# Attention rounds of four tiles and two score steps, on four score banks

## The reference

```
h = rmsnorm(x, g)
z = h @ w_in
y_lru = rg_lru(causal_depthwise_conv(u_lru, conv_w, conv_b), ...)
o_cmp, p_cmp = cmp_attention(q, compress(kc), compress(vc))   # 31 compressed blocks
o_slc = slc_attention(q_rot, rope(ks), vs, idx, ok)           # selected blocks
o_win = win_attention(q_rot, rope(kwn), vwn)                  # window of 512
y_nsa = gates[0] * o_cmp + gates[1] * o_slc + gates[2] * o_win
y = concat(y_lru * silu(g_lru), y_nsa * silu(g_nsa))
return x + y @ w_out
```

## Time and profile before

| | us |
|---|---|
| median of 3 runs | 549.22 (549.05 to 549.28) |
| the profiled execution's own time | 550.92 |
| its span, first to last instruction | 549.1 |
| attention of layer 0, from the second score step to the last `W` | 139 to 246 |
| attention of layer 1 | 404 to 527 |

### The profile page before, as it was taken

One profiled execution on the slowest core, in us unless ns is written; L12 is line 12 of the kernel. 1 busy time (PEld: TensorE's weight loads), 2 busy tenths in 40 slices (PEclk: granted clock), 3 DMA queues, 4 the chain that ended last, 5 costly groups with the idle time before them and its releaser, 6 DMA issues.

```text
span 549.1 us, 8550 instructions
## 1 busy us (share of the span) xinstructions
PE 529.4 (96%) x3055; PEld 389.4 (71%) x3055; DVE 397.2 (72%) x633; ACT 293.3 (53%) x595; POOL 87.5 (16%) x105
## 2 busy tenths in 40 slices
PE   8999999999999999899999999999999998999995
PEld 7777868778666656558887787777776665666674
DVE  3596996789977787754747499668978689569642
ACT  5756733626666555533634773562475554446532
POOL 4101101120111011103520110013111111113000
PEclk9999999999999999999999999999999999999999
DMA  9776483455212433412333846626432233112113
GB/s 268 204 214 174 96 206 84 103 119 143 70 34 52 102 73 78 99 36 75 84 95 95 218 124 156 125 59 142 108 116 65 62 87 82 34 40 59 38 39 115
DMA packets 108186, 57.25 MB, mean 104 GB/s; under 512 B 42721, under 2 KB 106353, under 8 KB 108145
## 3 DMA queue, kind: packets, MB, share of 16 engines
q1 hardware_dynamic: 104992, 52.25, 37.9%
q0 software_dynamic: 1536, 3.15, 2.4%
q10 hardware_dynamic: 1616, 1.32, 0.8%
HBM read 44.12 MB, written 2.10 MB: 84 GB/s over the span
## 4 chain that ended last, share of the span: by engine, by line
PE 64%; DVE 18%; issue 6%; SPq 5%; DMA 3%; ACT 3%; POOL 1%; POOLq 0%; DVEq 0%; ACTq 0%
PE z_ps L1630 10%; PE z_ps L1632 10%; PE z_ps L1631 10%; PE s_ps L1706 5%; PE o_ps L1771 3%; PE o_ps L1630 3%; PE t_ps L1729 3%; PE o_ps L1632 3%; PE o_ps L1631 3%; PE a_ps L1771 3%; DVE mn L1512 2%; DMA probsT<-swp 2%; DVE probs L1396 2%; PE t_ps L1734 2%; DVE w_lo L1224 1%
## 5 line engine op out<-in xcount | busy, mean ns | idle before, releaser
L1152 ACT ACTIVATE probs<-s_ps,mn 128x128 f32<-128x128 f32 (+3 forms) x128 | 66.7, 527 | 76.1 <-DVE mn L1512 75.6
L1630 PE MATMUL z_ps<-h_hi,w_hi 128*128 128x512 f32 x248 | 101.3, 409 | 0.0
L1632 PE MATMUL z_ps<-h_hi,w_lo 128*128 128x512 f32 x248 | 97.0, 391 | 0.0
L1631 PE MATMUL z_ps<-h_lo,w_hi 128*128 128x512 f32 x248 | 96.8, 390 | 0.0
L974 ACT ACTIVATE w_hi<-stage 128x1024 fp32r<-128x1024 f32 x54 | 57.3, 1060 | 60.4 <-PE z_ps L1632 35.4
L1512 DVE TENSOR_REDUCE mn<-s_ps 128x1 f32<-128x384 f32 (+3 forms) x88 | 52.3, 636 | 30.7 <-PE s_ps L1714 30.5
L939 POOL TENSOR_TENSOR w_lo<-stage,w_hi 128x1024 fp32r<-128x1024 f32 x13 | 31.2, 2401 | 180.6 <-ACT w_hi L974 180.6
L1630 PEld LDWEIGHTS z_ps<-h_hi,w_hi 128*128 128x128 f32 x248 | 46.6, 188 | 14.0 <-issue 4.2
L1224 DVE TENSOR_TENSOR w_lo<-stage,w_hi 128x1024 fp32r<-128x1024 f32 x41 | 50.1, 1222 | 5.5 <-ACT w_hi L974 4.8
L1632 PEld LDWEIGHTS z_ps<-h_hi,w_lo 128*128 128x128 f32 x248 | 46.5, 188 | 10.3
L1631 PEld LDWEIGHTS z_ps<-h_lo,w_hi 128*128 128x128 f32 x248 | 46.7, 188 | 8.4 <-issue 0.2
(11 more groups left out here) (248 smaller groups left out, 984.3 us busy)
## 6 DMA issues: line engine op xcount, KB each, us to landing
stage<-in_w_in SPq DMA_DIRECT2D x27, 512.0 KB, 4.1
stage<-in_w_in SPq DMA_DIRECT2D x34, 256.0 KB, 3.9
probsT<-swp SPq DMA_DIRECT2D x112, 64.0 KB, 2.1
stage<-in_cmp_k_w SPq DMA_DIRECT2D x8, 512.0 KB, 4.0
stage<-in_cmp_v_w SPq DMA_DIRECT2D x8, 512.0 KB, 4.2
stage<-in_w_out SPq DMA_DIRECT2D x8, 512.0 KB, 3.5
stage<-in_w_out SPq DMA_DIRECT2D x16, 256.0 KB, 4.0
swp<-E POOLq DMA_DIRECT2D x48, 64.0 KB, 2.3
```

The lines of the kernel that those rows point to most:

```text
L1152: act.activation(probs[:, 4 * pair + 2 * g + r, c0:c0 + W], s_ps[g][:, at * W:(at + 1) * W], ACT.Exp, scale=-1.0, bias=mn[:, m % 2, g, at: ...
L1630: pe.matmul(bank, w_hi[:, slot, at:at + P], x_hi, start=first, stop=False)
L1631: pe.matmul(bank, w_hi[:, slot, at:at + P], x_lo, start=False, stop=False)
L1632: ins = pe.matmul(bank, w_lo[:, slot, at:at + P], x_hi, start=False, stop=last)
```

## The change

The attention stage is written anew. `tile_rounds`, `SECONDS` and `put_later` go; `SETS` holds twelve sets of four tiles, and a round now has four tiles and two score steps `a` and `b`. The two steps of a round use different banks: `a` uses both `s_ps`, `b` uses `z_ps[1]` and `t_ps[1]`. That leaves one bank, `z_ps[0]`, for pieces and one, `t_ps[0]`, for turns; the last two sets may also turn into both `s_ps`. The first tile of ten sets a layer goes by `D` (issued by SP at a step of its own, `DX`), the other 38 are turned by TensorE and all copied by ScalarE. All `w_lo` of this stage are made by VectorE, none by GpSimd. `probsT` has four slots and two areas for coefficients. The probabilities that a round computes are turned two rounds later. The order of all small steps is given by tables and by the place in the round.

```diff
-N_STAGE, N_RING, N_PT, N_FAR, N_E, N_SWP = 4, 3, 2, 2, 6, 2
+N_STAGE, N_RING, N_SLOT, N_E, N_SWP = 4, 3, 4, 6, 2
...
+N_START = KT
+PIECES = (((8, 4),) + ((4, 0),) * 9 + ((2, 0), (0, 0)), ((8, 4), (4, 4)) + ((4, 0),) * 10)
...
+GATED_AT = {6: 0, 8: 1, 10: 2}
...
+SETS = tile_sets()
+FAR = {tiles[0] for tiles in SETS[2:]}
...
+    add(("S", step))
+    close()
+    add(("MX", step, 0), ("MX", step, 1))
+    split("HI")
+    add(exps(step, 0), exps(step, 1), *tanhs, ("CS2",), *silus)
...
+        for at, turn in enumerate(turns):
+            add(turn)
+            if at == 0:
+                if late:
+                    add(late)
+                add(*(("O", *group) for group in ended(n - 1) if group not in COEFS_AT[n]))
+                add(*(("K", *group) for group in COEFS_AT[n]))
+            if at == 1:
+                add(*tanhs)
+                if n < len(SETS) and SETS[n][0] in FAR:
+                    add(("D", SETS[n][0]))
+                add(*silus)
+                tanhs, silus = [], []
+                if n in GATED_AT:
+                    add(("Y", GATED_AT[n]), ("YH", "n", GATED_AT[n]))
+            fill(share[at])
...
+            add(("S", a), ("MX", a, 0), ("MX", a, 1))
+            close()
+            add(("S", b), ("MX", b, 0), ("MX", b, 1), exps(a, 0), exps(a, 1), exps(b, 0))
+            late = exps(b, 1)
...
+        add(*rest, *(("W", key) for key in tiles))
...
+        score_banks, turn_banks = [s_ps, [z_ps[1], t_ps[1]]], [t_ps[0], *s_ps]
...
+            if plan.turn_bank[n]:
+                eng.wait_ge(exp_ok, plan.exps[per_layer(plan.steps, plan.turns[n][0] + 1) - 1])
...
-                    if plan.low[split][0] == "pool":
-                        hi, lo = split_into(split)
-                        pool.wait_ge(hi_split, hi_count(split))
-                        pool.tensor_tensor(lo, stage_of(plan.split[split]), hi.bitcast(F32), ALU.subtract).then_inc(low_pool, 1)
...
-                elif kind == "T":
-                    key = (st[1], *st[2])
-                    if key[1] != "B" and st[2] in SECONDS:
-                        n, rows = turn_no[key], P if key[1] == "P" else NC
-                        dve.wait_ge(t_full, n + 1)
-                        dve.tensor_copy(probsT[0:rows, wait_near_slot(dve, key), :], t_ps[n % 2][0:rows, :]).then_inc(pt_dve, 1)
...
-                if m >= 1:
-                    pe.wait_ge(exp_ok, plan.exps[m])
+                if m >= 2:
+                    pe.wait_ge(exp_ok, plan.exps[m - 1])
+                if m == per_layer(plan.steps, l) + 1:
+                    who, count = plan.freed(plan.z, plan.z_before[l])
+                    pe.wait_ge(z_free[who], count)
+                    pe.wait_ge(gates_read, 4 * CT * (l + 1))
```

More of the change, by code:

```diff
@@ L136, in attention, with add @@
         pieces += [("G", l, t, c, p) for t in range(TT - 1) for c in range(2) for p in range(CT)]
-    taken = 0
+    steps = score_steps()[1:]
+    s, taken, closing, splits, tanhs, silus, finals = [], 0, [], 0, [], [], []
+    def add(*some):
+        s.extend((st[0], l, *st[1:]) for st in some)
     def fill(n):
-        nonlocal taken
-        out = []
+        nonlocal taken, splits
         for st in pieces[taken:taken + n]:
-            out.append(st)
+            s.append(st)
             if st[0] == "G":
@@ L151, in fill @@
+                splits += st[2] == KT - 1
+                splits += st[1:] == (("OL", DEPTH - 1, KT // 2 - 1), KT - 1)
         taken += n
[L152 to L205, removed]
@@ L207, in attention @@
-    ahead = score_steps()
-    turned = {key[1:4]: n for n, tiles in enumerate(rounds) for key in tiles if key[0] == "P"}
-    def score(n):
-        if not ahead:
-            return []
-        if any(turned[unit] > n for b, pair, _ in parts(ahead[0]) for unit in probs_before(ahead[0][0], b, pair)):
-            return []
-        return [ahead.pop(0)]
-    def exps(step):
-        return [("EX", l, step, n) for n in range(2)]
-    ahead.pop(0)
-    second = ahead.pop(0)
-    s = [*fill(2), ("TURN", l, LAST), ("TURNE", l, LAST), *fill(FIRST_PIECES[l] - 2), ("S", l, second), ("MX", l, second, 0),
-         ("MX", l, second, 1), *fill(SECOND_PIECES), *exps(second), ("CS2", l)]
@@ L245, in attention, with close, split, exps @@
-    return put_later(s + fill(len(pieces)))
+    def close():
+        for st in closing:
+            add(st)
+            if st[0] == "FE":
+                tanhs.append(("TANH", st[1]))
+                silus.append(("SG", st[1]))
+            if st[0] == "GE" and st[2] == 1:
+                add(("FMEAN", st[1]))
+                finals.append(("FSCALE", st[1]))
+        closing.clear()
+    def split(kind):
+        for _ in range(splits):
+            add((kind,))
+    def exps(step, half):
+        return ("EX", step, half)
@@ new lines, in ended @@
+    def ended(n):
+        last = {}
+        for at, tiles in enumerate(SETS):
+            for key in tiles:
+                last[(key[1], 2) if key[0] == "C" else key[1:3]] = at + 1
+        return [group for group in GROUPS if last[group] == n]
+    step = steps.pop(0)
+    fill(2)
+    add(("TURN", LAST), ("TURNE", LAST))
+    fill(N_START - 2)
+    add(("S", step))
[3 more added lines that the diff above has]
+    add(exps(step, 0), exps(step, 1), *tanhs, ("CS2",), *silus)
@@ L248, in schedule @@
+    i = TT - 1
+    add(*(("O", *group) for group in ended(len(SETS))), ("Y", i), ("YH", "n", i), ("YL", "n", i))
+    while taken < len(pieces):
+        fill(CT if taken % CT == 0 else CT - taken % CT)
+        split("HI")
+        lows, splits = splits, 0
+        close()
+        add(*(("LO",) for _ in range(lows)))
+        if len(finals) > 1:
+            add(finals.pop(0))
+    add(*finals)
+    return s
 def schedule():
@@ L1366, in _ @@
                 if kind in ("ON", "LO") and split < len(plan.split):
[L1367 to L1368 removed]
+                    split_lo(split)
                     split += 1
```

250 lines of the change are left out of this document (123 added, 127 removed).

## The result

The changed kernel takes **557.5 us** (median of 4 runs, 556.0 to 558.3) against 549.25 for the kernel before (median of 4, 549.05 to 550.3): a ratio of 1.0143, 95% interval 1.0117 to 1.0169. It is slower by some 8 us. The prediction said slower and named 551.9; it missed by 5.6 us, and the time lies above its range.

A forecast was written before the change was run, and what follows sets the result against it. TensorE, busy 96%, was taken to bound the kernel through its waits. New waits +16.1, matmuls 0 and removed waits -13.3 gave +2.8 us, added to the median 549.22 and rounded down: 551.9 us, range 547.6 to 555.6.

The forecast's parts named there:

- the cost in matmuls: TensorE in attention: eight more turned tiles cost 4.1 us, fewer weighing groups save 3.8; taken as 0, between -2 and +2.
- What the change removes: TensorE's waits in both attention stages and one clock fall: all 13.3 us gone, at the least half, 6.7.
- VectorE at nothing: VectorE gains 17 splits of 1.22 us, loses 20 copies and eight transposes; these balance, so costed at nothing.
- The new waits: TensorE waiting in attention, mostly for ScalarE's copies of turned tiles: +16.1 us together.
- fourth tile, rounds 1 and 2: Last weighing waits 1.4 us for a copy behind six exponentials, four times in all: +5.8 us (3 to 8).
- opening: Second turn of each layer waits 1.7 us for ScalarE's copy of the first: +3.4 us (2 to 4).
- one-piece gaps and `YH`: 24 turns one piece apart wait 0.15 us each, +3.6; `YH` delays third copies in rounds 6, 8, 10, +1.8.
- bank of the first chunk: Layer 0: the second score step waits for the first chunk's bank to be evicted: +0.8 us.
- second turn of round 11: Layer 0: this turn needs `s_ps`, so it waits for the very last exponential: +0.7 us.
- The third, that the clock falls in the new waits: Rival: TensorE's new waits of 1.4 to 1.7 us bring falls costing 1.7 us each; two give 555 us; chance 0.1.
- The first rival: ScalarE reaches the opening and fourth-tile copies a microsecond sooner, shrinking those waits to 1.4 and 1.8 us; 546 us; chance 0.2.
- the fourth, VectorE: Rival: VectorE is half a microsecond late in each of 16 long rounds, 8 us; 560 us; chance 0.05.

The follow-up runs named there:

- b_dve: The kernel before with one part of the change alone: VectorE makes every `w_lo` of attention, GpSimd none; 546.35 us, ratio 0.9922.
- a_pool: The changed kernel with one part undone: GpSimd makes the `w_lo` of attention again; 557.7 us, ratio 1.0134.
- e_fourth: The changed kernel with the fourth tile of rounds 1 and 2 turned between the two score steps, so copied before the six exponentials; 548.45 us, ratio 0.9963.
- e_open: The changed kernel with ScalarE's copy of each layer's first turned tile ahead of the second score step's exponentials; 554.3 us, ratio 1.0082.
- e_cover2: The changed kernel with unread extra matmuls in TensorE's long idle times: 13 at each of six places, 16 at the far tile; 554.3 us, ratio 1.0077.
- e_b_far: The changed kernel with coefficient turns of rounds 3, 4, 6, 8, 10 between score steps and the last round's far tile weighed last; 554.35 us, ratio 1.0062.
- e_4_shift8: e_fourth with 8 extra matmuls of 256 bf16 columns before layer 0's attention opening; 549.8 us, ratio 0.9996.
- e_4_shift: e_fourth with 16 extra matmuls of 256 bf16 columns before layer 0's attention opening; 550.5 us, ratio 1.0004.

## Why the prediction was wrong, point by point

**What bounds the kernel** was right in the main: waits of TensorE and its clock account for every experiment. Between the two kernels the spacing of the matmuls moved the time too, see the cost in matmuls.

**What the change removes.** The waits of score steps went, all of them. Their size, 11.6 us, can be checked only together with the cost in matmuls: the changed kernel's span without falls, 552.6, less its new waits of 19.3 (below) is 533.3; the kernel before, 549.05 less 1.0 for its fall less 11.6, is 536.4. The step that failed in the sum is the next one. I took 1.7 us for the fall of the clock out of the profiled span, and then laid the sum on the median of 549.22. But that median was of runs without this fall: the time of a run stands 1.7 to 2.3 us over its span, mostly 1.8, so 549.2 is a span of some 547.4 (an inference, since no clock is known of those three runs), while the profiled 549.1 held the fall. In 21 later runs of the kernel before, seven spans lie at 547.2 to 548.0 with a clock of 0.998 or 0.999, and all but one of the others at 548.5 to 549.9 with 0.994 to 0.998. So **the same 1.7 us were taken off twice.** "Profiling adds about 1.7 us outside what changes" was the wrong reading of a difference that was the clock itself. Half of its length was also too much for this fall: it cost 1.0 us (b_dve).

**The cost in matmuls**, 0 between -2 and +2: the two sums above leave -3.1 us. Added up by starts and less waits and falls, over both layers, turns take 3.2 us more (forecast 4.1) and weighing 2.4 less (forecast 3.8). A term was missing: the score steps take 20.1 and 20.3 us a layer in the kernel before and 18.9 in the changed one, where two of them follow each other without other work between, 2.6 less. That is -1.8 counted and -1.3 not placed, so the cost lay at the low bound or beyond it. VectorE at nothing: right, by b_dve and a_pool, but for the far tile below.

**The new waits**, 16.1 us, were measured at 19.3, which the matmuls' -3.1 cancels by luck:

| place | forecast | measured | by |
|---|---|---|---|
| fourth tile, rounds 1 and 2 | 5.8 | 6.2 | e_fourth |
| opening | 3.4 | 3.8 | e_open |
| one-piece gaps and `YH` | 3.6 + 1.8 | 3.8 + 2.6 | starts in e_cover2: 18 waits of 0.16 and six of 0.46 to 0.82; moving 20 turns gave 3.6 back |
| bank of the first chunk | 0.8 | 0.8 | timeline after: 10.96 us between two score steps, 10.11 in layer 1 |
| second turn of round 11 | 0.7 | 0 | timeline after |
| far tile of round 12 | none | 2.1 | idle time and its edge; e_b_far gave 1.05 back |

The last row was missed. I had written that a far tile is sent a round ahead, and didn't follow VectorE's queue in round 11 of layer 0, where the transpose stands behind a `w_lo` of 1.22 us, two outputs and the coefficients, with no pieces left to cover the DMA:

```profile
247.60 0.43 DVE L1548 COPY probsT<-coef 128x512 f32<-128x512 f32 x1
247.94 1.10 DVE L1534 STREAM_TRANSPOSE swp<-probs 128x512 f32<-128x512 f32 x1
```

In round 11 the last exponential was in time, so that 0.7 never came.

**The rivals.** The third, that the clock falls in the new waits, is what happened, and it had 0.1. It was argued from one row: waits of 1.3 us brought no fall, one of 2.18 did. The sum took six new waits of 1.4 to 1.7 us, between the two, and put nothing in for the clock; this is the second step that failed, and the larger one, 3.2 us by e_cover2. There were seven such waits, with the far tile's 2.0. Its price of two falls, 3.4 us, was a fair estimate. The first rival (ScalarE reaches the copies sooner) is out: the fourth tile's copy in round 1 ran from 4.96 to 5.55 us after the score step's start, as laid out, and the second turn of the opening came at 6.4 instead of 6.2 us. So is the fourth, VectorE. Beside the third rival stood a rule of the Trainium skill ("TensorE: Matmul & The Clock Gate", section "A second HAM failure mode: psum-queue depth-cycling"), by which the many short waits on one bank would make the clock swing. The trace agrees with the row and not with it at this size: e_cover2 has all 24 waits on that bank (0.16 us, and six of up to 0.8) and no fall in attention, and in every profile the falls in attention began in or within 2 us behind an idle time of 1.5 us or more.

**The sum of the error.** Laid on the profiled execution's own time, 550.9, with what was measured, the sum is 550.9 - 11.6 - 1.0 + 19.3 - 3.1 = 554.5 us (-3.1 is itself what was left of two such sums), against 554.3 measured without falls in e_cover2. The forecast of 551.9 lacked 1.7 by the base, 0.7 by the price of the old fall, 0.1 by rounding and 0.1 by new waits and matmuls together, which were each 3 us off in opposite directions. The falls in the new waits add 3.2. Of what the prediction said would show it, all waits were found at their places, with 1.56 us at the fourth tiles (idle time and its edge) for 1.4 and 1.86 at the opening for 1.7, and score steps no longer wait for exponentials.

## What to carry to other kernels

When a wait is traded for another, write down what stands ahead of the releasing instruction in its engine's queue: here four copies behind six exponentials each, and two behind eight, with the falls that came at them, ate what a better layout had won, and moving them ahead, with three smaller moves, made the kernel 2.2% faster than the old one. Before subtracting a disturbance that a profiled execution shows, see whether the median has it at all, by comparing the granted clock and span of each run. And price an idle time of TensorE of 1.5 us or more, as they were here, with a chance of a fall of the clock on top of its length.

## What the runs showed of the hardware

- The lower clock costs at most half its length: 1.0, 1.2, 1.4, 1.6 and 1.7 us for falls of 3.4 us, 2.7 and 2.9 for 6.8, each as the difference of the same stretch with and without it.
- An idle time of 2.0 us with the same matmuls around it was followed by a fall in one profiled execution (e_4_shift8) and by none in two (e_fourth, e_4_shift); idle times of 1.0 to 1.3 us (the kernel before, b_dve) were followed by none. With the idle times filled by matmuls that nothing reads there was no fall before the program's end in the profile of e_cover2, and the clock was 0.998 or 0.999 in its five runs.
- Score steps that follow each other directly take less of TensorE's time than single ones: 18.9 us a layer instead of 20.1 and 20.3.
- VectorE's operation on 128x8 elements, stretched to 1.85 and 2.36 us by a `w_lo` of GpSimd in one order, took 0.43 us at most in another with the same 17 operations on GpSimd: whether the two meet is a matter of order. The Trainium skill, "SBUF — State Buffer", section "Who interferes with whom", gives the rule that they exclude each other; the runs add that its price here ran from 4.4 us to nothing. The rule's bound in the prediction, 40 us of VectorE held, was far off: the stretched operations of the kernel before came to 14 us.
